# Choosing the experts of a mixture: part of the ranking before the last logits, the last rows by TensorE, the second gather in the next block

## The reference, cut to what matters

```python
x = x + gt1 * y                                   # y: output projection
h2 = modulate(rmsnorm(x, g_norm2), sh2, sc2)      # the rows that the experts read
lg = h2 @ w_rg                                    # (1024, 4) group logits
g_sel = argmax(lg)                                # one group of 4
le_sel = (h2 @ w_re) of that group                # 8 expert logits
top_w, top_i = top_k(softmax(le_sel), 2)          # two experts of 8
eid = g_sel * 8 + top_i                           # each token goes to 2 of 32 experts
# tokens are sorted by expert; each expert works on its own rows:
ys = (silu(xb @ w_gate[e]) * (xb @ w_up[e])) @ w_down[e]
# and the result is added back with the gates, then a last rmsnorm
```

## Time and profile before

| what | value |
|---|---|
| median of 3 runs | 1263.9 us (1263.22 to 1266.0) |
| profiled execution: span from first to last instruction | 1263.3 us |
| PE busy | 1220.1 us, 97% of the span |
| DVE busy | 959.5 us |
| mean granted TensorE clock | 0.990 of full |
| block of the experts begins | 648.0 us from the span's start |

### The profile page before, as it was taken

How to read it: one execution, slowest core, us unless ns; L and a number is a source line. 1 busy time by engine, 2 the same in 40 slices (tenths; PEclk the granted TensorE clock), 3 DMA queues, 4 the chain that set the end, 5 groups by cost and what they waited for, 6 DMA issues and landing times. The chain is left out here.

```text
span 1263.3 us, 18788 instructions
## 1 busy us (share of the span) xinstructions
PE 1220.1 (97%) x7332; PEld 1013.2 (80%) x7332; DVE 959.5 (76%) x1173; ACT 681.5 (54%) x819; POOL 257.5 (20%) x193
## 2 busy tenths in 40 slices
PE   4799999999999999999989999999999999999997
PEld 1799888888788887888778888888888888788883
DVE  1756554432578888666789999999999999999977
ACT  3932212111456666422256777777777777677734
POOL 0000000001100000100020634535355272622110
PEclk9899999999999999999989999999999999999999
DMA  9649844435566775431379999999999999999949
GB/s 380 252 178 311 286 138 142 170 121 169 185 221 185 156 189 133 151 110 51 137 264 358 379 386 392 375 389 380 382 385 377 385 375 395 382 363 378 384 150 359
DMA packets 96620, 344.36 MB, mean 273 GB/s; under 512 B 18522, under 2 KB 46866, under 8 KB 68883
## 3 DMA queue, kind: packets, MB, share of 16 engines
q1 hardware_dynamic: 75603, 311.91, 67.8%
q10 hardware_dynamic: 11696, 14.44, 3.9%
q0 software_dynamic: 9232, 16.80, 3.6%
HBM read 314.24 MB, written 39.34 MB: 280 GB/s over the span
## 5 line engine op out<-in xcount | busy, mean ns | idle before, releaser
L2262 DVE TENSOR_TENSOR w_low<-raw,w_high 128x2048 fp32r<-128x2048 f32 x128 | 291.7, 2299 | 6.0 <-ACT w_high L2194 5.1
L2194 ACT ACTIVATE w_high<-raw 128x2048 fp32r<-128x2048 f32 x128 | 240.8, 1908 | 4.9 <-PEq L1388 3.8
L2076 PE MATMUL p_gu<-w_high,x_high 128*128 128x512 f32 x504 | 202.5, 402 | 0.0
L2078 PE MATMUL p_gu<-w_high,x_low 128*128 128x512 f32 x504 | 197.2, 391 | 0.0
L2077 PE MATMUL p_gu<-w_low,x_high 128*128 128x512 f32 x504 | 196.3, 390 | 0.0
L2262 DVE TENSOR_TENSOR w_low<-arena,w_high 128x2048 fp32r<-128x2048 f32 x62 | 142.6, 2303 | 25.5 <-ACT w_high L2194 25.5
L2134 POOL DMA_INDIRECT y_rows<-arena,row x31 | 66.9, 2158 | 311.1 <-DVE arena L2293 309.6
L2194 ACT ACTIVATE w_high<-arena 128x2048 fp32r<-128x2048 f32 x62 | 118.2, 1906 | 0.0
L2078 PEld LDWEIGHTS p_gu<-w_high,x_low 128*128 128x128 f32 x504 | 94.6, 188 | 20.9
L2077 PEld LDWEIGHTS p_gu<-w_low,x_high 128*128 128x128 f32 x504 | 94.9, 188 | 18.0
L2076 PEld LDWEIGHTS p_gu<-w_high,x_high 128*128 128x128 f32 x504 | 95.2, 189 | 17.7
(11 more groups left out here) (426 smaller groups left out, 2532.1 us busy)
## 6 DMA issues: line engine op xcount, KB each, us to landing
raw<-in_w_gate SPq DMA_DIRECT2D x64, 1024.0 KB, 7.9
raw<-in_w_up SPq DMA_DIRECT2D x64, 1024.0 KB, 8.1
arena<-in_w_down SPq DMA_DIRECT2D x62, 1024.0 KB
raw<-in_w_ada SPq DMA_DIRECT2D x24, 1024.0 KB, 7.6
x<-qk_rows SPq DMA_DIRECT2D x6, 1664.0 KB, 8.3
raw<-in_w_chunks SPq DMA_DIRECT2D x9, 1024.0 KB, 5.7
qk_rows<-x SPq DMA_DIRECT2D x18, 512.0 KB, 2.6
mod<-x ACTq DMA_DIRECT2D x48, 128.0 KB, 3.2
```

The lines of the kernel that those rows point to most:

```text
L2076: pe.matmul(dst, high, w_high, start=start, stop=False)
L2078: return pe.matmul(dst, low, w_high, start=False, stop=stop)
L2194: act.activation(x.high[i % SPLITS][:], x.raw[b][:, :], ACT.Copy).then_inc(high_ok, 1)
L2262: dve.tensor_tensor(x.low[i % SPLITS][:], x.raw[home(n, j)][:, :], x.high[i % SPLITS][:], ALU.subtract).then_inc(low_ok, 1)
```

## The change

1. The ranking is split at tile 5. `rank_early` writes the counts of tiles 0 to 4 to a part of `p_y[0]`, and their contribution to the later tiles to `p_r`. DVE makes the one-hot rows of the five tiles after tile 6 (`ones(one_early, early)`), their ranks ahead of the last tile's `move_x`, and their matches behind it. POOL and ACT make their codes, and PE sums their part of the list early. The same for tiles 5 to 7 is done after the last logits.
2. The last tile's rows of `h_rows` are no longer made on DVE. ACT makes eight diagonals of the scale (`scale_diagonals`) and one of the root (`root_diagonal`); PE multiplies the turned tile with them and adds the shift (`p_y[1]`); ACT moves the two halves with `rstd` as scale (`last_rows`) and stores them.
3. SP loads `raw[1]` and `raw[2]` when those products are done (`logits` at `NT + 3`), no longer at `scaled_last` and the last logits.
4. The second gather moves to the head of POOL's list in the experts' block; POOL copies the early one-hot rows and ranks to their place after the first gather.
5. The low part of chunk 0 moves to the experts' block, ahead of that of chunk 1, and the low part of chunk 2 behind the two splits of the rows.
6. The counts of `stay_awake`: choice 2 x 14 becomes 6, rank 12 becomes 10, list 24 becomes 16, rows 30 becomes 24.

```diff
-AWAKE_SUMS, AWAKE_MIX, AWAKE_CHOICE, AWAKE_RANK, AWAKE_LIST, AWAKE_ROWS = 4, 3, 14, 12, 24, 30
+AWAKE_SUMS, AWAKE_MIX, AWAKE_CHOICE, AWAKE_RANK, AWAKE_LIST, AWAKE_ROWS = 4, 3, 6, 10, 16, 24
...
+        scale_diag, root_diag = s.raw[1][:, D:2 * D], s.raw[1][:, 0:P]
+        p_early = p_y[0][:, 1, 0:EARLY_CHOICE * NE]
...
-                sp.wait_ge(scaled_last, 1)
+                sp.wait_ge(logits, NT + 3)
                 load_chunk(sp, a, s.raw[1], s.loaded[1], 0, 1)
-                sp.wait_ge(logits, NT + 1)
                 load_chunk(sp, a, s.raw[2], s.loaded[2], 0, 2)
...
-                pool.wait_ge(chosen, 4)
-                for d in range(2):
-                    pool.tensor_tensor(code[:, :, d, :], one_e.rearrange("p (k e) -> p k e", e=NE),
-                                       digits[:, 2 * NT * d:2 * NT * (d + 1)].unsqueeze(2).to_broadcast([P, 2 * NT, NE]), ALU.mult).then_inc(coded, 1)
+                def tile_digits(part, ones):
+                    tiles = code.rearrange("p (k i) d e -> p k i d e", k=2)
+                    for k in range(2):
+                        pool.tensor_tensor(tiles[:, k, part, 0, :], ones[:, k], digits[:, part].unsqueeze(2).to_broadcast([P, part.stop - part.start, NE]),
+                                           ALU.mult).then_inc(coded, 1)
+                pool.wait_ge(chosen, 3)
+                tile_digits(early, one_early)
+                pool.wait_ge(chosen, 5)
+                tile_digits(late, one_e.rearrange("p (k i e) -> p k i e", k=2, e=NE)[:, :, late, :])
                 for b in range(2):
                     pool.wait_ge(h_out[b], 16 * NT // 2)
                 pool.wait_ge(listed_ok, 1)
-                for n in range(2):
-                    gather(pool, a, s, n)
-                pool.wait_ge(coded, 4)
+                gather(pool, a, s, 0)
+                c.step(pool.tensor_copy(one_e.rearrange("p (k i e) -> p k i e", k=2, e=NE)[:, :, early, :], one_early[:]))
+                c.step(pool.tensor_copy(rk.rearrange("p (k i) -> p k i", k=2)[:, :, early], rk_early[:]))
...
+                def scale_diagonals():
+                    act.wait_ge(scaled2, NT - 1)
+                    for k in range(KD):
+                        act.activation(scale_diag[:, k * P:(k + 1) * P], s.ident[:], ACT.Copy, scale=s.scale2[:, k:k + 1]).then_inc(act_made, 1)
+                def root_diagonal():
+                    act.wait_ge(rooted, 2 * NT + 1)
+                    act.activation(root_diag, s.ident[:], ACT.Copy, scale=root[:, 2, NT - 1:NT]).then_inc(act_made, 1)
+                def last_rows():
+                    act.wait_ge(scaled_last, 1)
+                    act.wait_ge(h_out[(NT - 1) % 2], 16 * (NT // 2 - 1))
+                    for h in range(2):
+                        act.wait_ge(logits, NT + 2 + h)
+                        act.activation(xrow[(NT - 1) % 2][:, h * 512:(h + 1) * 512], p_y[1][:, h, :], ACT.Copy,
+                                       scale=rstd[:, 2, NT - 1:NT]).then_inc(scaled_last, 1)
+                    act.wait_ge(scaled_last, 3)
+                    act.dma_start(a.h_rows[(NT - 1) * P:NT * P, :], xrow[(NT - 1) % 2][:]).then_inc(h_out[(NT - 1) % 2], 16)
+                def row_digits(part, ones):
+                    tiles = code.rearrange("p (k i) d e -> p k i d e", k=2)
+                    for k in range(2):
+                        act.activation(tiles[:, k, part, 1, :], ones[:, k], ACT.Copy, scale=digits[:, 2 * NT:2 * NT + 1]).then_inc(act_made, 1)
+                    act.activation(tiles[:, 0, part, 2, :], ones[:, 0], ACT.Copy, scale=-1.0).then_inc(act_made, 1)
...
+                    if n == NT - 2:
+                        scale_diagonals()
+                        act.wait_ge(chosen, 3)
+                        row_digits(early, one_early)
+                root_diagonal()
                 move_logits(NT - 1)
...
+                last_rows()
                 act.wait_ge(exps_in, 1)
                 act.activation(gdif[:], gdif[:], ACT.Exp).then_inc(exps, 1)
-                store_x(NT - 1)
                 first_high(0)
-                act.wait_ge(chosen, 4)
-                act.activation(code[:, 0:NT, 2, :], one_e[:, 0:NT * NE].rearrange("p (i e) -> p i e", e=NE), ACT.Copy, scale=-1.0).then_inc(coded, 1)
+                act.wait_ge(chosen, 5)
+                row_digits(late, one_e.rearrange("p (k i e) -> p k i e", k=2, e=NE)[:, :, late, :])
+                first_high(1)
                 act.wait_ge(exps_in, 2)
                 act.activation(wexp[:], wexp[:], ACT.Exp).then_inc(exps, 1)
-                first_high(1)
...
+                    if n == NT - 1:
+                        dve.wait_ge(placed, 1)
+                        dve.wait_ge(added, 2 * NT + 2)
+                        ranks(rk_early[:], one_early[:], early)
                     move_x(n)
+                    if n == NT - 2:
+                        ones(one_early, early)
+                        dve.sem_inc(chosen, 1)
                     if n == NT - 1:
-                        scale_last()
+                        dve.wait_ge(h_out[0], 16 * NT // 2)
+                        matches(rk_early, early)
                         norm_x(n)
...
+                pe.wait_ge(act_made, SPLIT_ROWS + KD + 4)
+                pe.wait_ge(added, 2 * NT + 1)
+                for h in range(2):
+                    pe.matmul(p_y[1][:, h, :], root_diag, shift2[:, h * 512:(h + 1) * 512], start=True, stop=False)
+                    for k in range(4 * h, 4 * h + 4):
+                        last = pe.matmul(p_y[1][:, h, (k % 4) * P:(k % 4 + 1) * P], xt[(NT - 1) % 2][:, k, :], scale_diag[:, k * P:(k + 1) * P],
+                                         start=False, stop=(k % 4 == 3))
+                    last.then_inc(logits, 1)
+                pe.wait_ge(coded, 2)
+                pe.wait_ge(matched, 2)
+                for k in range(2):
+                    lists(early, k)
+                stay_awake(pe, p_y[0][:, 0, :], s.ident[:], AWAKE_CHOICE)
+                pe.wait_ge(chosen, 4)
+                last = rank_late()
+                last.then_inc(placed, 1)
+                stay_awake(pe, p_y[0][:, 0, :], s.ident[:], AWAKE_RANK)
+                pe.wait_ge(act_made, SPLIT_ROWS + KD + 7)
                 pe.wait_ge(coded, 4)
...
             steps = Counter(pool, over_ready)
+            gather(pool, a, s, 1)
             pool.wait_ge(x_turned, 1)
...
+            split(0, 0)
             split(0, 1)
-            split(0, 2)
             x_split_first(0)
             x_split_second(0)
+            split(0, 2)
```

115 lines of the change are left out of this document (63 added, 52 removed).

## The result

The changed kernel took 1266.49 us in the median of 20 runs (1263.83 to 1270.66), the kernel before 1264.51 us in 20 runs beside it (1262.13 to 1266.66). The ratio is 1.0019, with a 95% interval of 1.0010 to 1.0028: 0.19% slower, just inside the 0.2% bound of the text. Two later sets of 12 runs gave 1.0006 (0.9994 to 1.0018) and 1.0019 (1.0005 to 1.0033). The forecast was 1261.7 us with a range to 1264.3, so the time fell outside, on the other side.

What follows compares the result with a forecast made beforehand. TensorE, busy 97% of the span, was taken as the bound, with 22.6 us of mostly identity turns ahead of the experts. Block end 2.8 us earlier minus 0.6 at the second expert gave 2.2: 1261.7 us, range 1259.6 to 1264.3.

Steps and rivals of the forecast that it cites:

- the two choices: DVE's ranking around the last logits: 0.25 us lost ahead, 2.8 less behind, tokens ready at 640.6 us.
- No cost, but no cover: ACT's late codes ready at 638.8 us, against the first late match at 638.9.
- its 641.2 for the tokens: Token time by the Trainium skill page, which adds 1.38 us of drain to ACT's table load; late codes then at 640.2.
- The last rows: TensorE's products for the last tile's rows: bounds 1.7 and 3.4 us, 3.3 taken for mostly 1.2 GHz; store issued at 634.9.
- The end of the block before: In the kernel before, POOL's second gather ends the block at 647.99 us; the changed block ends at 645.2, 2.8 earlier.
- The store: Last store lands in 6.7 us, at 641.6, 1.0 behind the tokens; POOL's gather waits for it and starts at 642.6.
- rival C: TensorE starts the experts at 1.2 GHz; 24 turns take 4.3 to 5.1 us, 1.5 lost, time 1263.2 us; chance 0.22.
- 2 us idle: In C, TensorE's 16 turns end at about 643 us, leaving this gap ahead of the experts' block.
- the 17.2 of the sum: Second expert's first gates, in us behind the boundary, waiting for chunk 2; before 16.6, so 0.6 lost.
- Rival D: Low clock lasts through turns, rows and at least half the first 24 gate products; price 5.5 us, time 1267.2; chance 0.09.
- A: Likeliest case, as summed: the first gather waits for the store, not the list; 1260.9 to 1262.7 us; chance 0.40.
- three signs of being wrong: DVE's late chain not shrinking by 2.5 us, POOL's copies or codes held up behind DVE, second gather late for its rows.

Runs made afterwards that it cites:

- g1: Changed kernel with 48 turns of the identity behind the late token list in place of 16; median 1265.41 us, 1.0002 of the kernel before.
- after_again: The changed kernel, unchanged, profiled and timed a second time; 1.0006 of the kernel before.
- e1: Changed kernel with 48 turns of the identity behind the token list in place of 16, an earlier set of runs; 0.9983 of the kernel before.
- g3: Changed kernel with the last store issued by SP ahead of both chunk loads and 32 turns behind the list; 1263.84 us, 0.9994 of the kernel before.
- g2: Changed kernel with the last store issued by SP ahead of both chunk loads, turns left at 16; 1264.17 us, 0.9996 of the kernel before.
- d1: Changed kernel with the last tile's rows back on DVE, the store and the loads of chunks 1 and 2 at their old places; 0.9999 of the kernel before.
- f2: f1 with both gathers issued in the block of the choice again; 0.9987 of the kernel before.
- e4: Changed kernel with the last store issued by SP ahead of both chunk loads and 36 turns behind the token list; 0.9973 of the kernel before.
- e5: e4 with the store between chunks 1 and 2, ACT's late codes and second exponential each ahead of a high part; 0.9986 of the kernel before.
- f1: e4 with 32 turns behind the token list and ACT's order of e5; 0.9992 of the kernel before.
- e6: e5 with the low part of chunk 0 back in the block of the choice and chunk 2's ahead of the row splits; 1.0000 of the kernel before.

## Why the prediction was wrong, point by point

**What bounds the kernel; the two choices.** Right at the tokens, in part by luck. The last residual is 0.34 late (0.3), the early matches took 1.55 (1.85), the late logits are taken at 631.34 (631.7), and the tokens are ready at 640.52 (640.6). POOL's two copies took 0.67 us (0.85), the block ending 2.4 behind the gather's start. "No cost, but no cover" was wrong in its first half: ACT's codes came at 639.5 and not 638.8, while DVE's last match was done at 639.0, and the list waited for them some 0.35 us (2.8 when the last rows were late). DVE was ahead of the sum by about as much, so the two errors cancel in the 640.5. The exponential runs directly behind the load of its table (635.47 and 1.28, then 636.77), so the drain that the Trainium skill (ScalarE: Activation LUTs, What ACT_TABLE_LOAD costs) adds does not show, and its 641.2 for the tokens did not come.

**The last rows: mis-sized, and hidden by luck.** At 2.4 GHz I had 1.7 us, from the identity product at the end of the kernel. They took 3.6 (630.61 to 634.2) at a granted clock of 1.00 in that stretch; with the clock low in their first half, in g1, 5.2. The row was misread: its four records of 128x512 are two products in the code, since each f32 product is logged twice, so 1.7 us is the price of 1024 columns and not of 2048. The 3.3 that I took for the other clock hid this: the store was issued at 635.12, 0.2 late.

**The end of the block before.** The prediction has POOL's second gather end it, at 647.99. TensorE's turns did, in that one profile, and 17.4 behind J is what the other two profiles of that kind show. So some 0.6 of the 2.8 us counted as gain at this boundary is there only where the list's turns run at the low clock.

**The store: the step that failed first.** I took a landing of 6.7 us with 7.8 as the bound, "nearer to the row since two chunks are again ahead". It was 8.5, 8.7 and 8.7 in three profiles of this kernel, beyond my bound. In the kernel before, by SP's timeline, the chunks had been issued at 629.20 and 630.48, 3.5 and 2.2 us ahead of the store of the earlier trace rows; now they were 0.7 and 0.4 ahead, so nearly all of their 2 MB had still to move. I had counted the chunks ahead and not how much of them was left. By the queues' view the store's own packets began about 4.5 us behind its issue in the kernel before and 4.0 in the changed one; but then it had to share with 0.31 MB of the chunks there (637 to 640.5 us) and with 0.99 MB here (639 to 643.6). The store lands at 643.6, behind the second chunk at 643.5, though it is half as large. Issued first it took 3.0, between the two 6.4. The Trainium skill (DMA: Bandwidth & Descriptors, Queues, rings and completion order) says that a transfer's completion is written only after every earlier write of the same DMA engine, across its queues; the trace agrees as far as the order goes (0.1 us between the two landings), and that rule should have been among the rivals, with chunk 2's landing as its time. That the rule is what cost the time isn't shown: the store's own packets ran until 643 us. The gather starts at 644.57 and not 642.6, and the block ends at 646.95, 1.75 later than the sum.

**The head: rival C, and not the likeliest case.** I gave 0.22 to a low clock through the 24 turns, with turns of 4.3 to 5.1 and 1.5 us lost. They took 5.35, 5.35 and 4.62. The gap ahead of the boundary, "2 us idle" in the text, was 5.2, since the block ended later and the 16 turns earlier: the late store made the gap longer, and I had counted the two as independent. How much of the low clock the gap made isn't shown by this kernel alone, since in after_again the clock was low before it. With the clock held, in e1, the second expert's gates come 17.25 behind the boundary, with a wait of 0.90 for ACT: the 17.2 of the sum. In the changed kernel they come 18.8 behind it, without that wait: TensorE itself was late, and chunk 2's load was issued 10.1 behind the boundary (8.0 in the sum, 8.0 in g3). That is another 1.6. Rival D did not come: the first gate products ran at the full clock, 1.20 us for four.

**The account.** 1.75 and 1.6 make 3.35: a gain of 2.2 becomes a loss of 1.1, which is what the rows show (665.74 for 664.62). To 1261.7 they give 1265.05. The kernel before stood at 1264.5 in the runs beside it and not at 1263.9: 1265.7. The median was 1266.5, and 0.8 is left; by the second set of runs (0.8 us over before) nothing is left, by the third again about 1 us. A low clock during the last rows, as in g1, would put 1.9 us on the block's start in some executions; that it makes up the rest is only argued. The sum also stops at the second expert's gates. From there to the end the changed kernel's profile took 596.3 us and the one before 598.7, with 1.9 us of waits for gathered rows; over all profiles this rest lies between 595.7 and 599.7. So the account explains the head, and that the medians differ by a like amount agrees with it and doesn't prove it.

**The signs.** The wait for the store came, as named for A. Of the three signs of being wrong that I had named, none was the cause: DVE's late chain shrank by over 2.5, POOL's copies were cheap, and the second gather was in time.

**What stays open.** Not every microsecond at the gates is one in the time. In g2 the store gave 1.9 us at the boundary but only 0.6 at the second expert's gates of its profile (35.4 for 36.0), and 2.5 in the median. d1 is 2.5 us ahead of the changed kernel's first profile at these gates and 0.0007 in the ratio of the medians, 0.9 us (1.5 in the means); f2 is 4.3 ahead and between 0.0019 and 0.0032, 2.4 to 4.0 us. Part of it is chance later on: TensorE waited 2.57 us for a gather at 1048 us in g1, 2.46 in g2, and for none in the changed kernel's profile. Whether these waits have to do with the head I didn't find out. No version here is shown to beat the kernel before by much: e4 was at 0.9973, but g3, the same with four turns fewer, at 0.9994; e5 (0.9986) and f2 (0.9987) are 1.8 and 1.6 us under it, with intervals that reach 0.9996 and 1.0000.

## What to carry to other kernels

Issue a small store that someone waits for ahead of the large loads, not behind them; its landing went by how much of them was still to move at its issue, so moving a load later can make the store longer though the same transfers are ahead of it. When a wait ahead of a block's end grows, count again what keeps TensorE's clock up across it: here the late transfer also left TensorE idle for 5.2 us, and each had its price. Before a row is used as a price, count its records against the products in the code. And profile the kernel before twice: its own head moved by 0.57 us. Before work goes from an engine with a long chain to TensorE "in its idle time", ask what that work releases (here the store, two loads and the codes), and what it takes at the low clock.

## What was new of the hardware

- A 512 KB store took 2.9 to 3.0 us to land with nothing large ahead of it, 6.4 behind one 1 MB load and 8.5 to 8.7 behind two just issued. Behind the two, its own packets began 4.0 us after its issue.
- Each f32 product here is logged as two instructions (one `matmul` of 512 columns as x2, four of 128 as x8). At 2.4 GHz the two records of a product of 512 columns with the row's data took 0.94 us to the next group's start; the four records of the two products with the identity are 0.43 to 0.44 apart. Four products of 128 columns took 0.9 us to the next group's start.
- In the changed kernel the clock came back (0.92 from 652 to 654 us) behind nothing but turns of the identity, and it held in e1, where 48 of them and a gap of 1.71 us led to 24 at 2.81 us. The Trainium skill (TensorE: Matmul & The Clock Gate, Part 4: PE-mode transpose) does not count transposes as activity; these rows are against it, as the earlier trace rows was.
- Over all profiles, where TensorE had nothing for 0.4 to 1.7 us ahead of the boundary the turns behind it ran at 2.4 GHz (eight profiles); where the gap was 2.1 to 5.4 us they ran at 1.2 GHz in nine and at 2.4 GHz in one (f1, 2.68 us). What it did ahead of the gap differs among them, and in after_again the clock was low before it and through it, so these rows are no rule for the length of a gap.
- A gather of 128 rows holds POOL for 1.0 to 1.24 us alone and for 2.47 to 2.52 beside DVE's subtraction of two SBUF tensors (long in the changed kernel and e6, short in f2). The Trainium skill (GPSIMD Engine Reference, Specifications) names this contention, for DVE instructions with two SBUF inputs; the trace agrees.
